# One 512-column matmul for the high and low halves of the activations, summed when PSUM is read, and a 64-byte shift of two tensors

## The reference

```
x = x + 0.5 * swiglu(rms_norm(x, g[0]), ffn1_w_in, ffn1_w_out)   # 1024 -> 2 * 2816 -> 1024
h = rms_norm(x, g[1]);  x = x + mixer(h)                         # q, k, v, gates; then w_out
x = x + memory_cross_attention(rms_norm(x, g[2]), rms_norm(mem, g[3]), w_q, w_kv, ..., w_o)
x = x + 0.5 * swiglu(rms_norm(x, g[4]), ffn2_w_in, ffn2_w_out)
def swiglu(h, w_in, w_out):
    g, u = split_cols(h @ w_in, (D_FF, D_FF));  return (silu(g) * u) @ w_out
```

## Time and profile before

| | |
|---|---|
| median of 3 runs | 2417.03 us (2408.07 to 2423.74) |
| profiled execution | 2406.13 us, of which the span from first to last instruction is 2404.3 us |
| mean granted TensorE clock | 0.978 of full speed |
| TensorE matmul busy | 2291.9 us (95%), 18446 matmuls |
| VectorE (DVE) busy | 1537.7 us (64%) |
| ScalarE (ACT) busy | 1184.5 us (49%) |
| DMA | 393.27 MB, mean 164 GB/s |
| idle before `w_lo` on DVE, waiting for ACT's `w_hi` | 533.2 us in 598 waits |
| idle before `w_hi` on ACT, waiting for a unit's last matmul | 864.2 us in 593 waits |

### The profile page before, as it was taken

The page is one execution under the profiler, slowest core; times in us unless marked ns, Lnnn a source line. Parts: engine busy times, 40 slices in busy tenths (PEclk is TensorE's granted clock), DMA queues, the critical chain, the costliest instruction groups (busy, mean ns, idle before and its releaser), DMA issues.

```text
span 2404.3 us, 44793 instructions
## 1 busy us (share of the span) xinstructions
PE 2291.9 (95%) x18446; PEld 2197.9 (91%) x18446; DVE 1537.7 (64%) x2216; ACT 1184.5 (49%) x1747; POOL 129.8 (5%) x146
## 2 busy tenths in 40 slices
PE   6999998889999999998999999998999999998998
PEld 6999876879999999787999999986999999998998
DVE  5766647566666765776666666667665666666664
ACT  5644434555446544445554544444544544426543
POOL 2000000110001001000100000100100000001001
PEclk9999987899999999999999999999999999999999
DMA  7556422326555557343455655642655565543653
GB/s 236 190 180 185 149 70 93 106 88 198 184 189 184 189 185 228 106 144 120 141 194 183 196 183 180 219 141 72 192 184 182 180 191 180 162 141 106 194 188 110
DMA packets 383369, 393.27 MB, mean 164 GB/s; under 512 B 6512, under 2 KB 381424, under 8 KB 383040
## 3 DMA queue, kind: packets, MB, share of 16 engines
q1 hardware_dynamic: 381248, 383.30, 49.9%
q0 software_dynamic: 1920, 7.11, 1.0%
HBM read 389.34 MB, written 1.05 MB: 162 GB/s over the span
## 4 chain that ended last, share of the span: by engine, by line
PE 87%; DVE 6%; ACT 4%; issue 1%; POOL 1%; DMA 1%; SPq 0%; POOLq 0%; ACTq 0%; DVEq 0%
PE acc L531 25%; PE acc L535 25%; PE acc L532 24%; PE wide L674 2%; PE acc L549 2%; PE acc L551 2%; PE acc L550 2%; ACT w_hi L815 1%; PE wide L647 1%; DVE w_lo L1048 1%; DVE hn_lo L1080 1%; POOL t L1432 1%; PE wide L663 1%; DMA raw<-in_ffn_w_in 1%; PE wide L602 1%
## 5 line engine op out<-in xcount | busy, mean ns | idle before, releaser
L815 ACT ACTIVATE w_hi<-raw 128x1024 fp32r<-128x1024 f32 (+1 forms) x742 | 768.7, 1040 | 963.8 <-PE acc L535 864.2
L1048 DVE TENSOR_TENSOR w_lo<-raw,w_hi 128x1024 fp32r<-128x1024 f32 (+1 forms) x742 | 889.2, 1201 | 536.1 <-ACT w_hi L815 533.2
L531 PE MATMUL acc<-hn_hi,w_hi 128*128 128x256 f32 x3536 | 855.7, 283 | 37.3 <-DMA colc<-in_cols 18.3
L532 PE MATMUL acc<-hn_lo,w_hi 128*128 128x256 f32 x3536 | 846.2, 280 | 0.0
L531 PEld LDWEIGHTS acc<-hn_hi,w_hi 128*128 128x128 f32 x3536 | 671.2, 190 | 50.7 <-DMA colc<-in_cols 18.3
L532 PEld LDWEIGHTS acc<-hn_lo,w_hi 128*128 128x128 f32 x3536 | 671.5, 190 | 0.5
L535 PE MATMUL acc<-hn_hi,w_lo 128*128 128x256 f32 x3536 | 482.1, 279 | 0.0
L535 PEld LDWEIGHTS acc<-hn_hi,w_lo 128*128 128x128 f32 x3536 | 442.2, 189 | 0.0
L531 PE MATMUL acc<-hid_hi,w_hi 128*128 128x256 f32 x1408 | 334.5, 278 | 0.0
L532 PE MATMUL acc<-hid_lo,w_hi 128*128 128x256 f32 x1408 | 334.5, 278 | 0.0
L532 PEld LDWEIGHTS acc<-hid_lo,w_hi 128*128 128x128 f32 x1408 | 265.3, 188 | 0.0
(11 more groups left out here) (199 smaller groups left out, 2036.4 us busy)
## 6 DMA issues: line engine op xcount, KB each, us to landing
raw<-in_ffn_w_in SPq DMA_DIRECT2D x88, 1024.0 KB, 5.1
raw<-in_ffn_w_out SPq DMA_DIRECT2D x32, 1024.0 KB, 5.2
raw<-in_ffn_pre_w_gate SPq DMA_DIRECT2D x22, 1024.0 KB, 5.3
raw<-in_ffn_pre_w_up SPq DMA_DIRECT2D x22, 1024.0 KB, 5.3
raw<-in_ffn_post_w_gate SPq DMA_DIRECT2D x22, 1024.0 KB, 5.3
raw<-in_ffn_post_w_up SPq DMA_DIRECT2D x22, 1024.0 KB, 5.3
raw<-in_x_w_kv SPq DMA_DIRECT2D x16, 1024.0 KB, 5.4
raw<-in_ffn_pre_w_down SPq DMA_DIRECT2D x16, 1024.0 KB, 5.1
```

The lines of the kernel that those rows point to most:

```text
L531: nc.tensor.matmul(bank, wh[:, j, :], a_hi[:, u.k0 + j, :], start=u.first and j == 0, stop=False)
L532: nc.tensor.matmul(bank, wh[:, j, :], a_lo[:, u.k0 + j, :], start=False, stop=False)
L815: nc.scalar.activation(w_hi[:, u.slot, 0:u.nk, :], raw[:, u.raw % RING, 0:u.nk, P * u.half:P * u.half + P], ACT.Copy).then_inc(w_hi_ready, 1)
L1048: nc.vector.tensor_tensor(w_lo[:, u.slot, 0:u.nk, :], raw[:, u.raw % RING, 0:u.nk, P * u.half:P * u.half + P], w_hi[:, u.slot, 0:u.nk, :]. ...
```

## The change

For F units, the high and the low activations of one kind become one tile (`hn`, `mn`, `hid`, with a second axis of 2), and one matmul with 512 moving columns (2 x 256) takes `w_hi` against both. Its result fills a whole bank: the first 256 columns hold high x high, the second 256 low x high ("cross"). The `w_lo` pass (256 columns) still adds into the first half. In a fresh unit the `w_lo` matmul of row block j follows directly on its 512-column matmul, instead of standing in a pass at the end. T units are as before.

The two halves are added when the bank is read. ACT copies the second half to a new SBUF tile `cross` (`copy_cross`, 522 outputs), and DVE adds the first half and `cross` (`add_cross`) ahead of the operation that it did before, which now reads SBUF. For `mixout` and `xo` (48 outputs) ACT does nothing, and DVE adds each half to x in turn. `before_normed` (64 bytes) and `before_weights` (64 bytes) make `hn`, `mn` and (behind it) `hid` start 64 bytes past a multiple of 128, the split weights at one.

```diff
-        hn_hi = sb("hn_hi", [P, KB, T], F32R)   ... hn_lo, mn_hi, mn_lo
+        before_normed = sb("before_normed", [P, 16])
+        hn = sb("hn", [P, 2, KB, T], F32R)
+        mn = sb("mn", [P, 2, KB, T], F32R)
         raw = sb("raw", [P, RING, 8, CW])
-        apart = sb("apart", [P, 16])
+        before_weights = sb("before_weights", [P, 16])
+        cross = sb("cross", [P, BANKS, T])
+        def cross_ap(o):
+            return acc[:, o % BANKS, T:2 * T]
 # TensorE, unit(i), mode F
-                    for j in range(u.nk):
-                        ...
-                        nc.tensor.matmul(bank, wh[:, j, :], a_hi[:, u.k0 + j, :], start=u.first and j == 0, stop=False)
-                        nc.tensor.matmul(bank, wh[:, j, :], a_lo[:, u.k0 + j, :], start=False, stop=False)
-                    pe.wait_ge(w_lo_ready, i + 1)
-                    for j in range(u.nk):
-                        mm = nc.tensor.matmul(bank, wl[:, j, :], a_hi[:, u.k0 + j, :], start=False,
-                                              stop=u.last and j == u.nk - 1)
+                    both, bank = acc[:, u.out % BANKS, :].rearrange("p (s t) -> p s t", s=2), out_ap(u.out)
+                    def low(j):
+                        return nc.tensor.matmul(bank, wl[:, j, :], a[:, 0, u.k0 + j, :], start=False,
+                                                stop=u.last and j == u.nk - 1)
+                    for j in range(u.nk):
+                        if fresh:  ... wait for r_hi, r_lo as before
+                        nc.tensor.matmul(both, wh[:, j, :], a[:, :, u.k0 + j, :], start=u.first and j == 0, stop=False)
+                        if fresh:
+                            if j == 0:
+                                pe.wait_ge(w_lo_ready, i + 1)
+                            mm = low(j)
+                    if not fresh:
+                        pe.wait_ge(w_lo_ready, i + 1)
+                        for j in range(u.nk):
+                            mm = low(j)
 # ScalarE: called in take, residual (hid only) and ffn_up, ahead of split_after of the same unit
+            def copy_cross(i):
+                act.wait_ge(unit_done, i + 1)
+                o = units[i].out
+                nc.scalar.activation(cross[:, o % BANKS, :], cross_ap(o), ACT.Copy).then_inc(cross_out, 1)
 # VectorE
+            def add_cross(out, i, rows=slice(0, P)):
+                dve.wait_ge(unit_done, i + 1)
+                dve.wait_ge(cross_out, crossed[i])
+                o = units[i].out
+                return nc.vector.tensor_tensor(out, out_ap(o)[rows], cross[rows, o % BANKS, :], ALU.add)
 # take
-                        ins = nc.vector.tensor_tensor(dest_ap(i), ps, rstd[:, 0, :], ALU.mult)
+                        link(add_cross(dest_ap(i), i))
+                        ins = nc.vector.tensor_tensor(dest_ap(i), dest_ap(i), rstd[:, 0, :], ALU.mult)
 # residual
-                            link(nc.vector.scalar_tensor_tensor(hidf[:, k % 2, :], out_ap(u.out), scale, rstd[:, 0, :],
+                            link(add_cross(hidf[:, k % 2, :], n))
+                            link(nc.vector.scalar_tensor_tensor(hidf[:, k % 2, :], hidf[:, k % 2, :], scale, rstd[:, 0, :],
                                                                 ALU.mult, ALU.mult))
                             ...
-                            nc.vector.tensor_tensor(x[:, k, :], x[:, k, :], out_ap(u.out), ALU.add).then_inc(out_evac, 1)
+                            link(nc.vector.tensor_tensor(x[:, k, :], x[:, k, :], out_ap(u.out), ALU.add))
+                            nc.vector.tensor_tensor(x[:, k, :], x[:, k, :], cross_ap(u.out), ALU.add).then_inc(out_evac, 1)
 # ffn_up
                 def scaled(h):
-                    nc.vector.tensor_tensor(silu_g[:, h, :], out_ap(units[u0 + h].out), rstd[:, 0, :], ALU.mult)...
+                    link(add_cross(silu_g[:, h, :], u0 + h))
+                    nc.vector.tensor_tensor(silu_g[:, h, :], silu_g[:, h, :], rstd[:, 0, :], ALU.mult)...
                 def mul(h):
+                    link(add_cross(hidf[:, h, :], u0 + 2 + h))
+                    dve.wait_ge(silu_done, m0 + h + 1)
-                    nc.vector.tensor_tensor(hidf[:, h, :], silu_g[:, h, :], out_ap(units[u0 + 2 + h].out), ALU.mult)...
+                    nc.vector.tensor_tensor(hidf[:, h, :], silu_g[:, h, :], hidf[:, h, :], ALU.mult)...
```

More of the change, by code:

```diff
@@ L2 @@
 from contextlib import ExitStack
+from itertools import accumulate
 import numpy as np
@@ L182, in build @@
         freed.append((kind, count[kind]))
+    name_of = {i: name for name, l in lin.items() for i in range(l.u0, l.u1)}
+    crossed = list(accumulate(u.last and u.mode == "F" and (u.src == "hid" or name_of[i][:3] not in ("mix", "xo0", "xo1"))
+                              for i, u in enumerate(units)))
     last_of_load = {u.raw: i for i, u in enumerate(units)}
@@ L221, in build @@
         pos = sb("pos", [P, T], I32)
-        with nc.sbuf_tensor("hid_hi", [P, HB, T], F32R) as hid_hi, nc.sbuf_tensor("hid_lo", [P, HB, T], F32R) as hid_lo:
-            pass
+        cross = sb("cross", [P, BANKS, T])
+        with nc.sbuf_tensor("hid", [P, 2, HB, T], F32R) as hid:
+            hid_hi, hid_lo = hid[:, 0], hid[:, 1]
         work = sb("work", [P, 2 * HB, T])
@@ L450, in wait_free @@
                 eng.wait_ge((gate_evac, hid_mul, out_evac)[kind], n)
-        name_of = {i: name for name, l in lin.items() for i in range(l.u0, l.u1)}
         def dest_ap(i):
@@ L530, in unit @@
                             pe.wait_ge(r_lo, 8 * u.need + j + 1)
-                        nc.tensor.matmul(bank, wh[:, j, :], a_hi[:, u.k0 + j, :], start=u.first and j == 0, stop=False)
-                        nc.tensor.matmul(bank, wh[:, j, :], a_lo[:, u.k0 + j, :], start=False, stop=False)
-                    pe.wait_ge(w_lo_ready, i + 1)
-                    for j in range(u.nk):
-                        mm = nc.tensor.matmul(bank, wl[:, j, :], a_hi[:, u.k0 + j, :], start=False,
-                                              stop=u.last and j == u.nk - 1)
+                        nc.tensor.matmul(both, wh[:, j, :], a[:, :, u.k0 + j, :], start=u.first and j == 0,
+                                         stop=False)
+                        if fresh:
[6 more added lines that the diff above has]
+                            mm = low(j)
                 else:
@@ L822, in take @@
                         state.evac = freed[units[i].out][1]
+                        if units[i].mode == "F":
+                            copy_cross(i)
                     split_after(i)
@@ L871, in residual @@
                     u = units[n]
+                    if u.last and u.src == "hid":
+                        copy_cross(n)
                     if n < l.u1 - 1:
@@ L1058, in take @@
                     if name == "af":
-                        ins = nc.vector.tensor_tensor(forget_z(0), ps[0:8], rstd[0:8, 0, :], ALU.mult)
+                        link(add_cross(forget_z(0), i, slice(0, 8)))
+                        ins = nc.vector.tensor_tensor(forget_z(0), forget_z(0), rstd[0:8, 0, :], ALU.mult)
                     elif name == "ga":
-                        ins = nc.vector.tensor_tensor(t2[96:128, 6, :], ps[96:128], rstd[96:128, 0, :], ALU.mult)
+                        z = t2[96:128, 6, :]
+                        link(add_cross(z, i, slice(96, 128)))
+                        ins = nc.vector.tensor_tensor(z, z, rstd[96:128, 0, :], ALU.mult)
+                    elif u.mode == "F" and u.src == "mn":
+                        ins = add_cross(dest_ap(i), i)
                     elif u.src == "mn":
@@ L1157, in scaled @@
                 def scaled(h):
-                    dve.wait_ge(unit_done, u0 + h + 1)
-                    nc.vector.tensor_tensor(silu_g[:, h, :], out_ap(units[u0 + h].out), rstd[:, 0, :], ALU.mult)\
-                        .then_inc(gate_evac, 1)
+                    link(add_cross(silu_g[:, h, :], u0 + h))
+                    nc.vector.tensor_tensor(silu_g[:, h, :], silu_g[:, h, :], rstd[:, 0, :], ALU.mult).then_inc(gate_evac, 1)
                 def mul(h):
-                    dve.wait_ge(unit_done, u0 + 2 + h + 1)
-                    dve.wait_ge(silu_done, m0 + h + 1)
                     if m0:
@@ L1167, in mul @@
                         dve.wait_ge(hid_lo_ready, m0 - 1 + h)
-                    nc.vector.tensor_tensor(hidf[:, h, :], silu_g[:, h, :], out_ap(units[u0 + 2 + h].out),
-                                            ALU.mult).then_inc(hid_mul, 1)
+                    link(add_cross(hidf[:, h, :], u0 + 2 + h))
+                    dve.wait_ge(silu_done, m0 + h + 1)
+                    nc.vector.tensor_tensor(hidf[:, h, :], silu_g[:, h, :], hidf[:, h, :], ALU.mult).then_inc(hid_mul, 1)
                 def low_hid(h):
```

18 lines of the change are left out of this document (8 added, 10 removed).

## The result

The changed kernel took 2428.83 us (median of 6 runs, 2425.27 to 2434.20), the kernel before beside it on the same chip 2412.02 (6 runs). The ratio is 1.0086, with a 95% interval of 1.0051 to 1.0120: slower by 0.9%. I had forecast 2356 us. The profiled execution took 2427.64 us, its span 2425.8, against 2406.13 and 2404.3 before.

What follows compares the result with a forecast made beforehand. The prediction took TensorE, busy 95% of the span, as the bound. Its terms, 82 - 3 - 2 - 6 - 8 - 3 - 4 - 1 = 55 us, took 2406 us to 2351, plus 5 made 2356; range 2331 to 2400.

Steps and rivals of the forecast that it cites:

- the price of the 512-column matmul: F units: each of 5456 pairs at 231 ns becomes one matmul at 216 ns, a gain of 82 us.
- up to about 115 ns of array time, the weight load sets the pace: TensorE matmuls: 6 to 11 ns excess at 256 columns comes from the weight load, hidden above 200 ns of array time.
- The 512-column matmul costs what the pair costs: Rival, every F unit: no matmul gain, evictions still paid; 2433 us, 2438 as a median, 2460 at 236 ns; chance 0.08.
- one excess per matmul: Rival, F units: half the excess stays, 222 ns per 512-column matmul, gain 49 us; 2384 us, 2389 as a median; chance 0.16.
- its gain of 14 us: Matmul term by the Trainium skill's rule: pair 218.4 ns, 512-column matmul 215.8; the prediction set this aside for the trace.
- the units that gain nothing: Units woven into attention, where TensorE waits anyway: 154 units hold 18 us of the 82; 4 us lost.
- Seams after down projections: Seven seams: everything after the last bank comes 0.85 us later, nearly all absorbed; 0.3 us each, 2 us.
- Seams after `mixout` and `xo`: Six seams: DVE falls 1.3 us behind plus 0.45, the fresh unit absorbs 0.7; 1 us each, 6 us.
- Up projections: New evictions hidden under TensorE, except 1.5 us at each of two memory norms (networks 0 and 2); 3 us.
- Projections and mixers: About ten whole projections evicted before the next step, 0.85 us each, 8 us; attention with units woven in, 3 us.
- Addresses: Start addresses of activations and split weights moved, distance of 64 bytes kept: zero, with 12 us to either side.
- the 5 us added to get from 2351 to 2356: Whole kernel: 2351 us lies 11 us under the runs' median; a third of the pace-dependent matmuls gone, so 5 added.

Runs made afterwards that it cites:

- e1: TensorE alone, streams of matmuls in several formats, lengths and addresses, no other engine at work: float32r 512 columns 226.7 to 233.4 ns, 256 columns 113.4 to 120.0.
- e3: The changed kernel with the addresses of the kernel before: 2428.39 us, ratio 1.0022 to the kernel before.
- e4: The changed kernel without its new evictions, second half of the banks never read: 2407.10 us, ratio 0.9938 to the kernel before.
- e6: The changed kernel, but the projections are read once and leave out low x high activations: 2422.99 us, ratio 1.0026 to the kernel before.
- e2: The kernel before with only the new addresses: 2408.88 us, ratio 0.9961 to the kernel before.
- e8: TensorE alone, streams of 48 float32r matmuls of 256 columns behind a pause or different leading matmuls: 113.3 or 117.8 ns each.
- e11: Kernel before, old addresses, new fresh-unit order, four 256-column matmuls split into 128s in 29 units (the two runs ahead: one, two): 2385.98 us, ratio 0.9916.
- e5: The changed kernel with each 512-column matmul as two of 256, new evictions kept: 2425.77 us, ratio 1.0035 to the kernel before.
- e7: The kernel before with only the new addresses and the fresh unit's new order: 2403.88 us, ratio 0.9934 to the kernel before.

## Why the prediction was wrong

**The step that failed is the price of the 512-column matmul.** I took 216 ns from the float32 matmul of 256 columns, "because its row has the same array time and a weight load for every matmul". It measured 232 ns in the kernel and 227 to 233 alone, so the term of 82 us of gain, 5456 x (231 - 216), was worth nothing. 5456 x (346 - 331.5) = 79 us; with that the sum's 2351 us becomes 2430, against 2427.6 measured. The other terms were off by less, and to both sides, as told below.

**Why the row misled.** I matched array time and a weight load, and held constant neither the format nor the rate at which columns pass. A float32 column holds the array twice as long, and its 2.5 ns are those of bfloat16. The larger excess belongs to float32r (e1), and it was still 13 to 20 ns at 213.3 ns of array time, where I had put 2. The reading that "up to about 115 ns of array time, the weight load sets the pace" was wrong: bfloat16 with the same 128 x 128 loads ran at 109.2 ns, and if the 111.7 ns of the 128-column stream is the load's floor in float32r, it lies under both paces.

**The rival was written down.** "The 512-column matmul costs what the pair costs" gave 2433 for the profiled execution, and it took 2427.6. I gave it 0.08 for one row against it, and that row was not float32r. Its mechanism as I had put it (moving operand and weights read at once, all through the columns) is neither shown nor excluded. For it: the weights' start alone changes the 512-column stream by 6.7 ns. Against it: most of the excess stays with a quarter of the weights' columns, and with both starts at 0 it does not grow from 256 to 512 columns. The rival "one excess per matmul" does hold at that one layout, but with an excess of 13.3 ns, too much for any gain over the fast pace. The T units, at 117.8 ns, said only that two pieces cost no more, not where the excess is from.

**A rule that was at hand.** By the Trainium skill, "TensorE: Matmul & The Clock Gate", section "Back-to-back issue gap", columns at 2.4 GHz plus 2.5 ns, both sides of the sum would have been wrong by this kernel's format, but its gain of 14 us was nearer to the measured nothing than my 82. e1 shows the rule true for bfloat16 (215.8 and 109.2) and not for float32r.

**The evictions came out near their sum, in part by luck.** I had 27 us with the units that gain nothing; e3 against e4 gives 21. By place they differ:
- Seams after down projections: 2 us forecast. The stall of the earlier trace rows, 1.38 us, became 1.73, and so at all seven: 2.4 us. The net was right, as a loss of 0.97 us by the evictions (0.85 forecast) and a gain of 0.62 by the new order. I had one late copy and one late addition; it was two additions and little of the copy.
- Seams after `mixout` and `xo`: 6 us forecast, and this was wrong. TensorE's waits there, 0.36 to 0.53 us before, add up to 1.2 us instead of 2.7. The new order more than made up for the late additions. All seam waits together went from 12.3 to 13.3 us, and the `mixout` and `xo` stages from 145.7 to 144.3.
- Up projections: 3 us forecast. DVE and ACT covered nearly all the new work: 1003.3 us became 1004.8. But the kernel before had some of these stages at the slow pace; against e4, which has the same matmuls, they took 6.4 us more, 2.9 of it at the three seams behind down projections.
- Projections and mixers: 8 + 3 us forecast. Compared with e4 they took 12.5 more, part of it at the lower clock, which I had not counted at all. e6 could not settle that figure. Against the profiled kernel before it is 20.7; the other 8 are there in e4 too, without any new eviction, and its granted clock was 0.971 against 0.978. What causes them was not tested.

**Smaller terms.** Addresses, priced at zero within 12 us to either side: 0.4% faster in e2, nothing in the absolute time of e3. I had assumed that only the distance between the two starts counts; in e1 two layouts with the same distance of 64 differ by 4 ns at 512 columns. The `w_lo` pass, taken at the mean of both paces, 115.5 ns, ran at 114. And the 5 us added to get from 2351 to 2356 do not follow from "a third of the pace-dependent matmuls is gone", which leaves 7 of 11; with a constant 216 ns two thirds would be gone, which leaves 4.

**What stays open**: why float32r matmuls cost more than their array time and why the addresses change it, and what in the first matmuls of a stream chooses between 113.3 and 117.8 ns. e8 to e11 show that short matmuls move it, not how.

## What to carry to other kernels

Fewer, longer matmuls only pay if the excess over array time is known to be per instruction. Take two stream lengths in the same number format, at the same addresses, before a kernel is rebuilt on it; a row of another format with the same array time is no substitute. Where the same code runs at two paces, ask what chooses between them: here a few 128-column matmuls and a new order in the fresh units, which need no new eviction, gave 0.8 to 1.0%, while the whole change lost 0.2 to 0.9%. And in a seam, count every operation that the last two outputs put in the queue, not one.

## What the runs showed of the hardware

- Start to start at full clock, with a 128 x 128 load for each matmul: float32r took 113.3 to 120.0 ns for 256 columns, 176.5 for 384 and 226.7 to 233.4 for 512; bfloat16 took 109.2 for 256 and 215.8 for 512.
- The starts of weights and moving operand within 128 bytes changed the float32r figures (e1): both at 0 gave 120.0 ns for 256 columns and 226.7 for 512; weights at 64 and moving operand at 0 gave 113.3 or 117.8, and 233.4.
- A 256-column float32r stream in the kernels kept its pace until a stall or a matmul of another kind (without exception in the traces of the kernel before, e2, e5 and e7). After two or more 128-column matmuls it took the fast one in 11 of 11 streams in isolation; with eight in the kernel, all but 11 of the steady units did.
- A stream of 128 columns with a 128 x 128 load for each ran at 111.7 ns, more than twice its array time.
- Waits of 1.7 us in a busy stretch were followed, at two of seven seams in the changed kernel and four of seven in e6, by some 3 us or more at a granted clock of 0.5; 3 us of it cost about 1.5 us.
